# Gate units of a projection placed between the items of the second attention, its preparation moved ahead, and a small projection moved in front of the last gate phase

## What is computed

```python
proj = rms_norm(x, g_mix) @ w_in
(q_n, kc_n, vc_n, ks_n, vs_n, kw_n, vw_n, gate_n, q_m, k_m, v_m, gate_a, gate_b) = split(proj)
y_nsa  = nsa_mixer(...)     # compressed, selected and window attention, 8 heads, 3 weighted branches
y_moba = moba_mixer(...)    # causal attention, 8 heads
merged = sigmoid(gate_a) * (y_nsa @ w_up_nsa) + sigmoid(gate_b) * (y_moba @ w_up_moba)
x = x + merged @ w_out
gate, up = split(rms_norm(x, g_ffn) @ w_ffn_in)
x = x + (silu(gate) * up) @ w_ffn_out
x = x + sigmoid(rms_norm(x, g_ple) @ w_ple_gate) * (p @ w_ple_proj)
```

## Time and profile before

| | |
|---|---|
| median of three runs | 2462.63 us |
| the profiled execution: its own time, its span | 2465.48 us, 2464.2 us |
| PE busy, records | 2315.4 us (94%), 14610 |
| DVE busy, ACT busy, POOL busy | 1482.7 us (60%), 1068.6 us (43%), 120.2 us (5%) |
| mean granted TensorE clock | 0.934 |

### The profile page before, as it was taken

One profiled execution on the slowest core, in us unless ns is written; L12 is line 12 of the kernel. 1 busy time (PEld: TensorE's weight loads), 2 busy tenths in 40 slices (PEclk: granted clock), 3 DMA queues, 4 the chain that ended last, 5 costly groups with the idle time before them and its releaser, 6 DMA issues. The chain is left out here.

```text
span 2464.2 us, 35572 instructions
## 1 busy us (share of the span) xinstructions
PE 2315.4 (94%) x14610; PEld 2031.8 (82%) x14610; DVE 1482.7 (60%) x2461; ACT 1068.6 (43%) x1740; POOL 120.2 (5%) x83
## 2 busy tenths in 40 slices
PE   5999999999899999899999988969997999999997
PEld 3988889998898888898888985569996975588997
DVE  4765775667666676665577655635654544355554
ACT  4522225644652223663222454554544443334443
POOL 1000001100200000100000110010000010000000
PEclk9999999999899999999999987989997995589999
DMA  7555554455344564445555442015655420034553
GB/s 274 183 166 192 192 165 156 154 188 188 120 172 161 198 197 164 157 159 171 197 181 182 154 146 86 1 55 170 238 182 192 147 95 18 1 115 142 190 176 116
DMA packets 70654, 378.21 MB, mean 153 GB/s; under 512 B 7487, under 2 KB 12223, under 8 KB 43867
## 3 DMA queue, kind: packets, MB, share of 16 engines
q1 hardware_dynamic: 67824, 369.91, 43.7%
q10 hardware_dynamic: 2666, 6.02, 0.7%
HBM read 374.85 MB, written 1.05 MB: 153 GB/s over the span
## 5 line engine op out<-in xcount | busy, mean ns | idle before, releaser
L477 PE MATMUL ps_g<-h,w_hi 128*128 128x256 f32 (+1 forms) x4288 | 1006.6, 330 | 13.8 <-DVE h L916 9.8
L828 DVE TENSOR_TENSOR w_lo<-w_raw,w_hi 128x1024 fp32r<-128x1024 f32 (+2 forms) x614 | 689.5, 1124 | 466.0 <-ACT w_hi L1334 465.4
L1334 ACT ACTIVATE w_hi<-w_raw 128x1024 fp32r<-128x1024 f32 (+2 forms) x614 | 593.0, 969 | 626.0 <-PE ps_g L477 525.7
L477 PEld LDWEIGHTS ps_g<-h,w_hi 128*128 128x128 f32 x4288 | 731.3, 193 | 89.2 <-issue 13.6
L477 PE MATMUL ps_g<-h,w_lo 128*128 128x256 f32 (+1 forms) x2144 | 703.8, 328 | 0.0
L477 PE MATMUL ps_g<-hid,w_hi 128*128 128x256 f32 (+1 forms) x2368 | 496.5, 308 | 3.1 <-DVE y L971 2.1
L477 PEld LDWEIGHTS ps_g<-h,w_lo 128*128 128x128 f32 x2144 | 413.5, 193 | 35.6
L477 PEld LDWEIGHTS ps_g<-hid,w_hi 128*128 128x128 f32 x2368 | 387.4, 192 | 26.5 <-DVE w_lo L828 2.6
L477 PE MATMUL ps_g<-hid,w_lo 128*128 128x256 f32 (+1 forms) x1184 | 363.6, 307 | 0.0
L477 PE MATMUL ps_g<-b_h,w_hi 128*128 128x256 f32 x1504 | 276.4, 287 | 7.7 <-DVE b_h L916 7.3
L477 PEld LDWEIGHTS ps_g<-b_h,w_hi 128*128 128x128 f32 x1504 | 236.3, 193 | 10.9 <-issue 10.0
(11 more groups left out here) (238 smaller groups left out, 1856.1 us busy)
## 6 DMA issues: line engine op xcount, KB each, us to landing
w_raw<-in_gu SPq DMA_DIRECT2D x130, 1024.0 KB, 4.9
mod_raw<-in_w_mod SPq DMA_DIRECT2D x128, 512.0 KB, 3.7
w_raw<-in_conv_cu SPq DMA_DIRECT2D x16, 1024.0 KB, 4.9
w_raw<-in_dn00b SPq DMA_DIRECT2D x16, 768.0 KB, 4.2
w_raw<-in_dn01b SPq DMA_DIRECT2D x16, 768.0 KB, 4.2
w_raw<-in_dn10b SPq DMA_DIRECT2D x16, 768.0 KB, 4.3
w_raw<-in_conv_out SPq DMA_DIRECT2D x8, 1024.0 KB, 4.9
w_raw<-in_w_in_a SPq DMA_DIRECT2D x8, 1024.0 KB, 4.9
```

The costliest lines, as they stand in the source:

```text
L477: mm = pe.matmul(ps_g[:, 2 * (u % 2) + m, cs], w[wp][:, k, m * P:(m + 1) * P], acts[ap][:, k, cs], start=(k == 0 and n == 0), stop=(k == k ...
L828: dve.tensor_tensor(w_lo[u % 2][:, cols], w_raw[u % 2][:, cols], w_hi[u % 2][:, cols].bitcast(F32), ALU.subtract).then_inc(lo_made, 1)
L1334: act.activation(w_hi[u % 2][:, cols], w_raw[u % 2][:, cols], ACT.Copy).then_inc(hi_made, 1)
```

## The change

- **Gates between items.** `attention` on PE returns `third_of_step`: a third of a step is one item's scores, turn or output. The first unit of `w_in_d` stays in front; the other seven call `attend` before each of their 16 chunks (3 matmuls), which from chunk 8 of the second unit on (104 chunks) runs the next one to three of the 207 thirds. `beside_gates` puts the splits of these units and their way out of PSUM between the steps of DVE and ACT.
- **Banks.** A gate unit uses one bank (`own_bank`), scores have 2 banks and turned probabilities 2. Gates leave PSUM by a copy; the sigmoids are taken later, in `up_phase`, two of 128x512 for each of its units (`gates_made`).
- **Preparation moved up.** The same work lies between the units of `w_in_a`, `w_in_b` and `w_in_c`. The five small loads are issued after the norm's work instead of inside it, the five for `compress` behind the second unit of `w_in_a`. `compress` now takes the hidden weights as the stationary operand and `flat` as 30 moving columns, in 32 matmuls, so that nothing need be turned; one silu is taken for both.
- **The projection of p** goes ahead of `ple_gate`: three pairs before the sums of the last norm, the fourth behind them, into four banks where it stays. p is loaded by ACT after attention and split in the norm before the last feed-forward part. Each gate unit's sigmoid, product, sum and store follow it.

```diff
@@ -90,8 +90,8 @@
     phase("w_up", range(4), UNIT)
     phase("w_out", range(4), UNIT)
     ffn(4, "gu2", "dn2")
+    phase("ple_proj", range(1), UNIT)
     phase("ple_gate", range(4), UNIT)
-    phase("ple_proj", range(1), UNIT)
...
+    att1 = attention_plan(items1, hid1, 0, 0, [ps_g[:, j, :] for j in range(3)],
+                          [ps_g[:, 3, :], ps_s[:, 2, :], ps_s[:, 3, :]])
+    att2 = attention_plan(items2, hid2, len(items1), NC, [ps_g[:, j, :] for j in range(2)],
+                          [ps_s[:, 2, :], ps_s[:, 3, :]])
+
+
+
+    D_UNITS = phase_units("w_in_d")
+    STEPS3 = 3 * (len(items2) + 5)
+    CHUNK0 = 2 * NC // 2
+    CHUNKS = 2 * NC * (len(D_UNITS) - 1) - CHUNK0
+
+    def step_by(n, chunk):
+
+        return -(-(2 * NC * (n - 1) + chunk - CHUNK0) * STEPS3 // (3 * CHUNKS)) + 1
...
+            def third_of_step(n):
+                s, third = divmod(n, 3)
+                if third == 0 and s < N:
                     scores(s)
-                if 0 <= s - 3 < N:
+                if third == 1 and 0 <= s - 3 < N:
                     turn_probs(s - 3)
-                if 0 <= s - 5 < N:
+                if third == 2 and 0 <= s - 5 < N:
                     outputs(s - 5)
-            pe.wait_ge(i_kept, a.kept + a.items[-1].tile + 1)
+            return third_of_step
...
         def compress(kv):
             pe.wait_ge(flat_made, 8 * (kv + 1))
-            if kv:
-                pe.wait_ge(c_hidden, 1)
-            for jp in range(16):
-                mm = pe.matmul(ps_s[0:30, 1, 0:S], flat[:, kv, jp, :, :].rearrange("p g c -> p (g c)"),
-                               compress_w(kv, jp), start=(jp == 0), stop=(jp == 15))
+            pe.wait_ge(cw1_in, 16 * 5)
+            for m in range(2):
+                for jp in range(16):
+                    mm = pe.matmul(ps_s[:, 1, 60 * kv + 30 * m:60 * kv + 30 * m + 30],
+                                   compress_w(kv, jp)[:, m * P:(m + 1) * P],
+                                   flat[:, kv, jp, :, :].rearrange("p g c -> p (g c)"),
+                                   start=(jp == 0), stop=(jp == 15))
             mm.then_inc(c_first, 1)
...
         def projections():
-            feature_phase("w_in_a", h2, NC, 2, normed(6, X))
-            b = FIRST["w_in_b"]
-            feature_unit(b, h2, NC, 2)
-            token_unit(b + 1, h2)
-            c = FIRST["w_in_c"]
-            token_unit(c, h2)
-            token_unit(c + 1, h2)
+            a, b, c = phase_units("w_in_a"), phase_units("w_in_b"), phase_units("w_in_c")
+            for u in a[:3]:
+                feature_unit(u, h2, NC, 2, normed(6, X) if u == a[0] else None)
             branch_matmuls()
-            d = phase_units("w_in_d")
-            feature_unit(d[0], h2, NC, 2)
+            feature_unit(a[3], h2, NC, 2)
+            feature_unit(a[4], h2, NC, 2)
             sum_rows(range(4))
-            feature_unit(d[1], h2, NC, 2)
+            feature_unit(a[5], h2, NC, 2)
             branch_turn()
+            feature_unit(a[6], h2, NC, 2)
+            feature_unit(a[7], h2, NC, 2)
             sum_rows(range(4, 7))
-            feature_unit(d[2], h2, NC, 2)
-            compress(0)
-            feature_unit(d[3], h2, NC, 2)
+            feature_unit(b[0], h2, NC, 2)
             pe.wait_ge(br_copied, 1)
             spread_rows((0, 1, 2), 0)
-            feature_unit(d[4], h2, NC, 2)
+            compress(0)
+            token_unit(b[1], h2)
+            spread_rows((3, 4, 5), 6)
             compress(1)
-            spread_rows((3, 4, 5), 6)
-            feature_unit(d[5], h2, NC, 2)
+            token_unit(c[0], h2)
             spread_rows((6,), 12)
             swap((0, 1), 1, 12, 0)
-            turn_hidden()
-            feature_unit(d[6], h2, NC, 2)
             compress_second()
+            token_unit(c[1], h2)
+            kc_sum()
             swap((2, 3, 4), 0, 14, 2)
-            kc_sum()
-            feature_unit(d[7], h2, NC, 2)
+            feature_unit(D_UNITS[0], h2, NC, 2, one_bank=True)
+            kc_swap()
             swap((5, 6), 0, 14, 5)
-            kc_swap()
+            third_of_step = attention(att2)
+
+            def attend(chunk):
+
+                if chunk == 0:
+                    pe.wait_ge(kc_made, 1)
+                    pe.wait_ge(r_rotated, 7)
+                    pe.wait_ge(br_made, 1)
+                if chunk >= 0:
+                    for n in range(chunk * STEPS3 // CHUNKS, (chunk + 1) * STEPS3 // CHUNKS):
+                        third_of_step(n)
+            for n, u in enumerate(D_UNITS[1:]):
+                feature_unit(u, h2, NC, 2, None, lambda at, n=n: attend(2 * NC * n + at - CHUNK0), one_bank=True)
...
+                    if u == FIRST["w_up"]:
+                        pe.wait_ge(i_kept, NC + 4 * src + 4)
                     if src == 0:
-                        pe.wait_ge(evac, u - 1)
+                        pe.wait_ge(evac, u if u == FIRST["w_up"] else u - 1)
...
             for pair in range(NC // 2):
+                if pair == 3:
+                    sums(sum_in(8), X)
                 for m in (2 * pair, 2 * pair + 1):
                     for k in range(2):
                         for n, (wp, ap) in enumerate(PARTS):
-                            mm = pe.matmul(ps_g[:, pair, S * (m % 2):S * (m % 2) + S], w[wp][:, k, m * P:(m + 1) * P],
-                                           hid2[ap][:, k, :], start=(k == 0 and n == 0), stop=(k == 1 and n == 2))
-                mm.then_inc(pair_done, 1)
+                            mm = pe.matmul(proj[pair][:, S * (m % 2):S * (m % 2) + S], w[wp][:, k, m * P:(m + 1) * P],
+                                           p_r[ap][:, k, :], start=(k == 0 and n == 0), stop=(k == 1 and n == 2))
+                if pair == 2:
+                    mm.then_inc(half_done, 1)
+            mm.then_inc(unit_done, 1)
+            spread_out(sum_in(8), X)
+            for u in phase_units("ple_gate"):
+                feature_unit(u, h2, NC, 2, normed(8, X) if UNITS[u].ul == 0 else None, one_bank=True)
...
+        def beside_gates(step_):
+
+            for n, u in enumerate(D_UNITS):
+                if 0 < n < len(D_UNITS) - 1:
+                    if step_ == step_by(n, 2 * NC) + 1:
+                        turn_of(u)
+                    if step_ == step_by(n + 1, NC) + 1:
+                        low_ahead(u)
...
+                dve.wait_ge(gates_made, ul + 1)
...
         def second_loads():
             loads = [
+                (gate_n[:], t["gate_n"]),
+                (pos_i[:], t["positions"].partition_broadcast(P)),
+                (to_row[:], t["to_row"]),
+                (from_row[:], t["from_row"]),
+                (causal[:], t["causal"]),
+            ]
+            for dst, src in loads:
+                act.dma_start(dst, src).then_inc(loads2_in, 16)
+
+        def compress_loads():
...
+        def sigmoids(ul):
+            for tiles in (slice(2 * ul, 2 * ul + 2), slice(NC + 2 * ul, NC + 2 * ul + 2)):
+                ins = act.activation(gates[:, tiles, :], gates[:, tiles, :], ACT.Sigmoid)
+            ins.then_inc(gates_made, 1)
 
         def up_phase():
             for u in phase_units("w_up"):
                 ul = UNITS[u].ul
+                if ul < 3:
+                    sigmoids(ul + 1)
                 high_half(u + 2, 1)
                 act.wait_ge(merge_sum, ul + 1)
                 act.activation(h2[0][:, 2 * ul:2 * ul + 2, :], merged, ACT.Copy).then_inc(merge_hi, 1)
...
+        attention(att2, beside_gates)
+        turn_of(D_UNITS[-1])
+        act.wait_ge(evac, D_UNITS[-1] + 1)
+        sigmoids(0)
+        high_ahead(D_UNITS[-1])
+        act.dma_start(p_in, t["p"]).then_inc(p_there, 16)
```

More of the change, by code:

```diff
@@ L614, in attn_layer @@
             pe.wait_ge(rot_made, 6)
-            attention(att1)
+            third_of_step = attention(att1)
+            for n in range(3 * (len(items1) + 5)):
+                third_of_step(n)
+            pe.wait_ge(i_kept, NC)
             feature_phase("attn_o", hid1, NC, 2)
@@ L1021, in rotate1, with attention @@
             dve.tensor_tensor(dst, dst, m1, ALU.add).then_inc(rot_made, 1)
-        def attention(a):
+        def attention(a, behind=None):
             N = len(a.items)
@@ L1082, in attention @@
                     keep_low(s - 6)
+                if behind is not None:
+                    behind(s)
         def attn_layer():
@@ L1228, in projections @@
             dve.tensor_tensor(kc, kc, kc_tmp, ALU.add).then_inc(kc_made, 1)
+        def projections():
+            a, b, c = phase_units("w_in_a"), phase_units("w_in_b"), phase_units("w_in_c")
+            turn_of(a[0])
+            low_ahead(a[0])
+            dve.wait_ge(loads2_in, 16 * 5)
+            step(dve.tensor_copy(pos_f, pos_i[:]))
+            step(dve.tensor_scalar(ang, pos_f, vec("inv_freq"), None, ALU.mult))
+            turn_of(a[1])
+            low_ahead(a[1])
+            dve.wait_ge(gn_hi, 1)
```

(46 more changed lines are left out.)

273 lines of the change are left out of this document (116 added, 157 removed).

## The result

The changed kernel takes **2499.4 us** (median; 2491.33 to 2502.26) where the kernel before, measured beside it, takes 2462.5: a ratio of 1.0144, 95% interval 1.0128 to 1.0161. It is slower by 37 us; the forecast was 2417, 45 us faster. The profiled execution took 2502.26 us, its span is 2501.0.

The account below looks back on a forecast made before the run. PE was taken as the bound, at half clock rate in the second attention. Terms from -60.5 for attention to +20 switching and +14 clock summed to -45.2, 2420.3 from the profiled 2465.48, 2417 as median; range 2398 to 2448.

Parts of the forecast that it names:

- Left: 1.2 us: Ahead of second attention: PE's wait for the last rotation shrinks from 5.5 us to 1.2, change -4.5 us.
- Rival (a): In the mix: the clock falls at PE's wait before the first item and stays low, 2515 us; chance 0.12.
- The mix at full level: Second attention with interleaved gates: 69.3 attention + 39.3 gates + 20 switching = 129 us.
- the switching term: In the mix: each group of three gate matmuls between fp32 pieces costs 0.20 us, +20 in all, bounds +10 and +30.
- If the level stays full: Second attention: at the full clock level its work takes 69.3 us instead of 129.8, a gain of 60.5.
- +14 for the clock: Under both `compress`: the clock falls, work there and 3.4 us of the next unit run at half rate, +7 each.
- -1.7 for the old fall: Behind the second `compress` with `spread_rows`: the earlier 3.40 us at clock 0.50 goes away, -1.7 us.
- norm -2.1: Norm ahead of `w_in_a`: load issues move behind the norm, so the root no longer waits in ACT's queue, -2.1 us.
- end and projection -7.1: Kernel end: less work behind the last gate record, -6.0 us; projection fills PE's idle time in the norm, -1.0.
- The tail: Behind attention: 7.3 us of thin and up-projection records need 4.2 at full level, -3.1 us.
- Rival (c): In the mix: the softmax chain on DVE and ACT becomes the bound through bursts, 2434 us; chance 0.06.
- (e): In the mix: interleaving stalls PE on order, gates arrive late and the gain is eaten, 2455 to 2470 us; chance 0.03.

Follow-up runs that it names:

- experiment 2: Changed kernel with DVE's rotation before a split half: 2414.8 us; later first item plus five or two idle products PE waits for: 2500.2, 2413.6 us.
- Experiment 4: Two kernels without the wait: all gate units in one piece before attention, 2461.8 us; four of eight units interleaved, on the old `compress` shape, 2467.4 us.
- experiment 6: Changed kernel with each `compress` before its `spread_rows`: 2502.2 us; first item later plus the old `compress` shape: 2399.8 us.

## Why the prediction was wrong
- **The step that failed** is "Left: 1.2 us" in the wait ahead of attention. I had the chain ending 6.0 us after the unit and PE arriving at 4.9. PE arrived as forecast (4.8); the chain ended at 7.5 (1995.68 to 2003.15). The half of a split that the text counted began on DVE where it should, 1.8 us behind the unit (1997.45), but took 1.91 us, not 1.23; behind it came the rotation of the compressed keys (1.4, where it was counted at nothing), and only then the four products and sums, 2.5. The other half of a split in DVE's queue (1.21) ended before and cost nothing. The slow operations lie beside POOL's cosines, which themselves take 3.50 us instead of the 2.49 of the earlier trace rows. In the kernel of experiment 2 with the rotation first, the cosines have no split beside them and take 2.57, and L1213, ahead of them, 0.17 instead of 1.17:

```profile
2002.59 0.17 DVE L1213 TENSOR_TENSOR small<-small,rope 128x15 f32<-128x15 f32 x1
2002.81 2.57 POOL L1834 TENSOR_TENSOR qk<-qk,rope 128x512 f32<-128x512 f32 x2 [3.74 <-PE ps_s L695]
```

That the two slow each other is read from these traces and was not tried by itself.
- **A wait of 1.2 us was rightly taken for harmless**: 1.16 us idle left the clock at 1.00. With the wait at 0.36 us and all else as changed, the time is 2414.8, 2 us from the 2417 forecast. That it is so near is in part luck: the mix is 5 us shorter than the forecast had it, `compress` and the tail are 2 us dearer, and the untouched work ahead was 1.5 us longer in that execution.
- **Rival (a) is what happened**, at its place and by its mechanism, with a chance of 0.12; but the wait that it named, 1.2 us, would not have done it. Its price was too high: 98 us against 209.45 - 122.18 = 87.3, which is why it gave 2515 and not 2499. It should have had more: the wait was worked out from a chain of three engines whose error (1.5 us, 7.5 against 6.0) was larger than the wait it left, and the price was one-sided.
- **The mix at full level**: 122.2 us (chunk 8) from the first score to the last output, where the forecast gives some 127 for the same stretch: 129, less 2.8 for the 24 gate matmuls that stand ahead of it, plus 1.2 for the last outputs, which it counted to the tail. Starting 24 matmuls (2.8 us) later shortened it by 3.5, so eight groups fewer saved some 0.7, about 0.1 us a group: an estimate, at the lower bound (+10) of the switching term, not at 0.20. By it attention itself took 76 (122.2 - 36.5 for 312 gate records - 10), not 70.5 (69.3 and these outputs). That its items, most of them thinner than those of the earlier trace rows, gain less from the level would explain it, but was not tried.
- **"If the level stays full"** was argued from the first attention. Experiment 4 shows that this was no argument: the second does not hold it by itself. What holds it is the gates in between, with 2.0 to 2.2 thirds behind each group, and no row of before spoke for that.
- **`compress`**: +1 for the shape and +14 for the clock, -1.7 for the old fall, 13.3 in all; measured 42.1 us for both with the units behind them against 27.3, +14.8. The price of a record at the full level, 0.12, came out at 0.11, and its double at the low one too. The sum came out, the mechanism only in part: `spread_rows` in front is not needed for the fall (experiment 6), the clock stays down to the end of `compress` and 3.4 us beyond, and the old shape in the new place, 9 us cheaper, was never priced.
- **Small terms**: norm -2.1 as forecast; end and projection -7.1 as forecast (-6.0 - 1.0); the last gate record 4.8 us before the end (4.9). The tail, from the last output on, gave -1.3 (-1.1 in the kernel with the rotation first); of the -3.1 forecast 1.1 is the last outputs at the full level, so 2.0 stands against it. Rival (c) did not show: DVE and ACT wait for PE, not the other way. Nor did (e): the interleaving runs without stalls (PE busy 118.60 of 118.60 us with the later start).
- **The range**: 2398 to 2448 is not what the bounds add up to. All low ones together (switching -10, wait -1.2, `compress` -14) give 2392, all high ones (+10, +2.5, +6, +3 for the loads, +17 for the cover) 2456; the text does not say how it came to less. 2499 lies outside either.

## What to carry to other kernels
Where the granted clock is at its low level in a stretch with a never idle PE, ask what level the stretch is entered with and whether its own work can keep it: here dense work spread between thin pieces kept it (118.6 us at 1.00), the same work in one piece ahead of them did not (down after 5.3 us). A wait at the entry (2.8 us here) can then have the price of the whole stretch behind it (some 85 us); give it a margin as large as the error of the chain it was worked out from, or put a few microseconds of dense matmuls behind it.

## What the runs showed of the hardware
The same mixed steps run for over 190 us at 1.2 GHz or for 119 at 2.4 GHz, in either case to the end, by what stood ahead of them; a dense piece of 6.9 us in between changed the one into the other. PE's busy share says nothing of it (1.00 in both). PE idle for 1.16 us in front of the mix left the level alone, 2.79 us did not. Fp32 records with 128x128 weights and 30 moving columns took 0.11 us at the full level and 0.21 at the low one, and a piece of them behind a dense unit brought the clock down about 3 us after its start without PE being idle.
